# A decoder block with 32 experts on one core: whole 2 MB weight transfers in 16 KB rows, an eleventh buffer, and gather rows scaled on DVE

## The reference

```python
h = rms_norm(x, g_mix)
proj = h @ w_in                                  # 1024 x 9728: attention q/k/v, retention q/k/v/g, two gates
A = dilated window attention, three groups, 8 heads of 64
R = chunkwise retention, 4 heads, group norm, silu gate
x = x + (sigmoid(gA) * (A @ P_A) + sigmoid(gR) * (R @ P_R)) @ w_out
h2 = rms_norm(x, g_ffn)
# 4 expert groups of 8; the best group, the best 2 experts in it
y = sum over 32 experts e of
      gate[:, e] * ((silu(h2 @ w_gate[e]) * (h2 @ w_up[e])) @ w_down[e])
out = rms_norm(x + y, g_final)
```

## Time and profile before

| | us |
|---|---|
| median of 3 runs | 818.76 (817.61 to 819.12) |
| the profiled execution | 817.54 |
| its span | 815.8 |
| PE busy | 590.4 (72%) |
| PE weight loads | 420.7 (52%) |
| DVE busy | 248.7 (30%) |
| ACT busy | 198.7 (24%) |
| POOL busy | 20.7 (3%) |

### The profile page before, as it was taken

How to read it: one execution, slowest core, us unless ns; L and a number is a source line. 1 busy time by engine, 2 the same in 40 slices (tenths; PEclk the granted TensorE clock), 3 DMA queues, 4 the chain that set the end, 5 groups by cost and what they waited for, 6 DMA issues and landing times.

```text
span 815.8 us, 11861 instructions
## 1 busy us (share of the span) xinstructions
PE 590.4 (72%) x4469; PEld 420.7 (52%) x4469; DVE 248.7 (30%) x430; ACT 198.7 (24%) x292; POOL 20.7 (3%) x30
## 2 busy tenths in 40 slices
PE   3999999999999999955680780780770870960966
PEld 3999999999999998841320320320320320320311
DVE  6776574766664456460000000000000000000001
ACT  5454544565555433410000000000000000000001
POOL 3000000000000000120000000000000000000000
PEclk9999999999999999968795795795895895895888
DMA  7645526478786556889999999999999999999994
GB/s 209 163 112 144 155 80 181 133 235 247 241 263 199 182 187 228 329 358 378 415 414 422 415 415 421 417 415 421 418 415 419 419 415 419 419 417 418 419 412 175
DMA packets 111287, 255.82 MB, mean 314 GB/s; under 512 B 10017, under 2 KB 71457, under 8 KB 95649
## 3 DMA queue, kind: packets, MB, share of 16 engines
q1 hardware_dynamic: 109040, 255.36, 83.1%
q10 hardware_dynamic: 2224, 0.17, 0.2%
HBM read 254.45 MB, written 1.05 MB: 313 GB/s over the span
## 4 chain that ended last, share of the span: by engine, by line
PE 56%; DMA 21%; SPq 16%; DVE 2%; issue 2%; ACT 1%; DVEq 0%; ACTq 0%
PE ps L1040 56%; DMA ring<-in_w_down 20%; SPq L418 10%; SPq L427 6%; DMA gain<-in_g_mix 1%; ACT work L589 1%; DVE hn L717 1%; DVE rb L922 0%; DVE work L898 0%; PE ps L1119 0%; PE ps L1143 0%; DVE hn L1034 0%; ACT work L684 0%; DVE hT L725 0%; DVE split L693 0%
## 5 line engine op out<-in xcount | busy, mean ns | idle before, releaser
L1040 PE MATMUL ps<-store,work 128*32 128x512 f32 x128 | 75.1, 746 | 189.3 <-DMA ring<-in_w_down 189.2
L1040 PE MATMUL ps<-ring,work 128*32 128x512 f32 x896 | 188.4, 616 | 1.6 <-DVE work L972 0.9
L693 DVE TENSOR_TENSOR split<-ring,split 128x768 fp32r<-128x768 f32 (+2 forms) x132 | 120.5, 932 | 91.7 <-ACT split L541 91.1
L1040 PE MATMUL ps<-hT,split 128*128 128x256 f32 x1152 | 141.9, 285 | 2.0 <-DVE hT L725 2.0
L1040 PEld LDWEIGHTS ps<-hT,split 128*128 128x128 f32 x1152 | 140.3, 194 | 2.9 <-issue 2.4
L1040 PEld LDWEIGHTS ps<-store,work 128*32 128x32 f32 x128 | 15.8, 133 | 239.8 <-issue 224.7
L541 ACT ACTIVATE split<-ring 128x768 fp32r<-128x768 f32 (+2 forms) x132 | 107.1, 824 | 120.3 <-PE ps L1040 88.8
L1040 PE MATMUL ps<-mid,work 128*32 128x512 f32 x256 | 131.9, 671 | 0.0
L1040 PE MATMUL ps<-split,hT 128*128 128x256 f32 (+2 forms) x672 | 106.5, 316 | 0.0
L1040 PEld LDWEIGHTS ps<-split,hT 128*128 128x128 f32 x672 | 98.1, 190 | 4.4 <-issue 0.5
L972 DVE COPY work<-ps 128x512 f32<-128x512 f32 x8 | 5.5, 692 | 262.5 <-PE ps L1040 262.5
(11 more groups left out here) (175 smaller groups left out, 443.7 us busy)
## 6 DMA issues: line engine op xcount, KB each, us to landing
ring<-in_w_up SPq DMA_DIRECT2D x48, 1024.0 KB, 17.6
ring<-in_w_gate SPq DMA_DIRECT2D x42, 1024.0 KB, 21.6
ring<-in_w_in SPq DMA_DIRECT2D x96, 192.0 KB, 3.3
oRT_slot<-in_w_gate SPq DMA_DIRECT2D x16, 1024.0 KB, 20.7
mid<-in_w_up SPq DMA_DIRECT2D x16, 1024.0 KB, 14.7
store<-in_w_down SPq DMA_DIRECT2D x8, 2048.0 KB, 22.1
hT_slot<-in_w_down SPq DMA_DIRECT2D x8, 2048.0 KB, 26.7
mid<-in_w_down SPq DMA_DIRECT2D x32, 512.0 KB, 20.2
```

Source lines behind the costliest of these rows:

```text
L693: dve.tensor_tensor(split[:, s, 1, 0:n], raw(s, n), split[:, s, 0, 0:n].bitcast(F32), ALU.subtract).then_inc(lo_ready, 1)
L1040: return pe.matmul(o, lhsT=l, rhs=r, start=start, stop=stop, skip_group_check=shared)
```

## The change

- The source of the downs is laid out so that a partition takes four consecutive rows: 16 KB in one piece. The transposes of the hidden rows take every fourth column to match.
- Gates, ups and downs 0, 1, 2 are fetched whole (2 MB, rows of 16 KB). The first refill of the gates stays in halves. Down 3 comes in three pieces (1 MB in rows of 8 KB, then twice 512 KB in rows of 4 KB).
- An eleventh buffer, `spare`. `G_AT, U_AT, D_AT = (3, 4, 5, 10), (7, 0, 1, 2), (8, 9, 6, 0)`: gate 3 in the new one, down 2 in buffer 6, so only down 3 still shares (with up 1). Gate 3 of the first team is loaded in quarters in the retention loop, down 2 of the first team takes its place before the passes.
- SP waits for `gate_done` alone, and for `down_done1` alone; `down_half` is gone.
- `hn` is made by DVE in one instruction per tile, with root and gain; ACT's scaling and POOL's product are gone.
- `dynamic_dma_scratch_size=1024` makes room in SBUF.

```diff
+D3_PIECES = ((0, 2), (2, 3), (3, 4))
...
-    wd_v = w_down.rearrange("e (c p) d -> e p c d", p=P)
+    wd_v = w_down.rearrange("e (p c) d -> e p (c d)", p=P)
...
+        spare = sb("spare", [P, 4096])
...
-        G_AT, U_AT, D_AT = (3, 4, 5, 6), (7, 0, 1, 2), (8, 9, 7, 0)
+        G_AT, U_AT, D_AT = (3, 4, 5, 10), (7, 0, 1, 2), (8, 9, 6, 0)
...
                 quarter(5, wg_v[2][:, bass.ds(i * 1024, 1024)], i)
+                quarter(10, wg_v[3][:, bass.ds(i * 1024, 1024)], i)
...
+            def load_whole(p, view, at, js, loaded):
+
+                for j in js:
+                    sp.dma_start(slots[at[j]], expert(view, p, j)).then_inc(loaded, 16)
+
+            def load_last_down(p, n):
+
+                for m, (f, end) in enumerate(D3_PIECES):
+                    sp.wait_ge(up_done if m else up_half, n + 1)
+                    words = slice(f * D, end * D)
+                    sp.dma_start(slots[D_AT[3]][:, words], expert(wd_v, p, 3)[:, words]).then_inc(down3_loaded[m], 16)
...
+            def refill(p, q, n, first=False):
+
+                if first:
+                    for h, done in enumerate((gate_half, gate_done)):
+                        sp.wait_ge(done, 1)
+                        for j in range(TEAM):
+                            words = slice(h * 2048, (h + 1) * 2048)
+                            sp.dma_start(slots[G_AT[j]][:, words], expert(wg_v, q, j)[:, words]).then_inc(gate_loaded, 16)
+                else:
+                    sp.wait_ge(gate_done, n + 1)
+                    load_whole(q, wg_v, G_AT, range(TEAM), gate_loaded)
+                load_last_down(p, n)
+                load_whole(q, wu_v, U_AT, (0, 2, 3), up_loaded)
+                sp.wait_ge(down_done[1], n + 1)
+                load_whole(q, wu_v, U_AT, (1,), up_loaded)
+                load_whole(q, wd_v, D_AT, (0, 1, 2), down012_loaded)
...
+            passes = n_passes(sp)
+            refill(0, team_of(1), 0, first=True)
+            with sp.Fori(1, passes - 1) as n:
+                refill(team_of(n), team_of(n + 1), n)
+            load_last_down(NP - 1, passes - 1)
...
-            for t in range(TT):
-                act.activation(x2[:, t, :], x2[:, t, :], ACT.Copy, scale=rstd[:, 1, t:t + 1]).then_inc(x2_scaled, 1)
...
+            dve.wait_ge(s_gain, 32)
             for t in range(TT):
                 dve.wait_ge(rstd_done, TT + t + 1)
+                dve.scalar_tensor_tensor(hn[:, t, :, :], permuted(x2[:, t, :]), rstd[:, 1, t:t + 1], permuted(gain[:, :]),
+                                         ALU.mult, ALU.mult).then_inc(hn_done, 1)
...
-                    ins = pe.transpose(ps[:, 0, f * P:(f + 1) * P], hid[:, f * P:(f + 1) * P], ident[:, :])
+                    ins = pe.transpose(ps[:, 0, f * P:(f + 1) * P], hid[:, f:FF:FT], ident[:, :])
```

More of the change, by code:

```diff
@@ L242, in hybrid_block @@
         wr_ready = sem("wr_ready")
-        proj_done, x2_ev, x2_scaled = sem("proj_done"), sem("x2_ev"), sem("x2_scaled")
+        proj_done, x2_ev = sem("proj_done"), sem("x2_ev")
         raw_loaded = [sem(f"raw_loaded{s}") for s in range(CH)]
         hi_ready, lo_ready, chunk_used = sem("hi_ready"), sem("lo_ready"), sem("chunk_used")
[L246 to L249, removed]
+        gate_loaded, up_loaded = sem("gate_loaded"), sem("up_loaded")
+        down012_loaded = sem("down012_loaded")
+        down3_loaded = [sem(f"down3_loaded{m}") for m in range(len(D3_PIECES))]
         early = sem("early")
@@ L323, in parts @@
             return [split[:, s, a, 0:n].rearrange("p (k n) -> p k n", k=steps) for a in range(2)]
-        slots = [ring[:, s, :] for s in range(6)] + [oRT_slot[:, :], mid[:, :], store[:, :], hT_slot[:, :]]
-        G_AT, U_AT, D_AT = (3, 4, 5, 6), (7, 0, 1, 2), (8, 9, 7, 0)
+        slots = [ring[:, s, :] for s in range(6)] + [oRT_slot[:, :], mid[:, :], store[:, :], hT_slot[:, :],
+                                                         spare[:, :]]
+        G_AT, U_AT, D_AT = (3, 4, 5, 10), (7, 0, 1, 2), (8, 9, 6, 0)
         def n_passes(eng):
@@ L387, in quarter @@
             def quarter(slot, src, i):
-                sp.dma_start(ring[:, slot, bass.ds(i * 1024, 1024)], src).then_inc(early, 16)
+                sp.dma_start(slots[slot][:, bass.ds(i * 1024, 1024)], src).then_inc(early, 16)
             with sp.Fori(0, RET_HEADS) as i:
@@ L396, in _ @@
                 quarter(5, wg_v[2][:, bass.ds(i * 1024, 1024)], i)
-            for h in range(2):
-                sp.sem_inc(gate_loaded[h], 48)
+                quarter(10, wg_v[3][:, bass.ds(i * 1024, 1024)], i)
+            sp.sem_inc(gate_loaded, 64)
             with sp.Fori(0, GI) as i:
@@ L429, in _ @@
+            def load_last_down(p, n):
[3 more added lines that the diff above has]
+                    sp.dma_start(slots[D_AT[3]][:, words], expert(wd_v, p, 3)[:, words]).then_inc(down3_loaded[m], 16)
             sp.wait_ge(chunk_used, CH * (Q_WRET + 2))
-            for h in range(2):
-                load_halves(0, wg_v, G_AT, (3,), gate_loaded, h)
+            load_whole(0, wd_v, D_AT, (2,), down012_loaded)
@@ L432, in _ @@
             sp.wait_ge(b_ready, KT // 2)
-            for h in range(2):
-                load_halves(0, wu_v, U_AT, (0,), up_loaded, h)
+            load_whole(0, wu_v, U_AT, (0,), up_loaded)
             sp.wait_ge(lo_ready, CH * QUADS)
-            for h in range(2):
-                load_halves(0, wu_v, U_AT, (1,), up_loaded, h)
+            load_whole(0, wu_v, U_AT, (1,), up_loaded)
             sp.wait_ge(chunk_used, CH * QUADS)
-            for h in range(2):
-                load_halves(0, wu_v, U_AT, (2, 3), up_loaded, h)
@@ L441, in _ @@
-            for j in range(2):
-                load_down(0, j)
+            load_whole(0, wu_v, U_AT, (2, 3), up_loaded)
+            load_whole(0, wd_v, D_AT, (0, 1), down012_loaded)
             sp.wait_ge(hn_done, 2 * TT)
             sp.dma_start(gain[:, :], g_final.partition_broadcast(P)).then_inc(s_gain, 16)
[L446 to L451, removed]
+            def refill(p, q, n, first=False):
[13 more added lines that the diff above has]
+                load_whole(q, wd_v, D_AT, (0, 1, 2), down012_loaded)
@@ L453, in _, with team_of @@
             sp.wait_ge(sched_ready, 1)
             sp.wait_ge(order_ready, 1)
+            def team_of(n):
+                return sp.value_load(order[0:1, 0, bass.ds(n, 1)], min_val=0, max_val=NP - 1)
             passes = n_passes(sp)
[L456 to L469, removed]
@@ L653, in _ @@
                                ACT.Copy).then_inc(hT_act, 1)
-            for t in range(TT):
-                act.wait_ge(rstd_done, TT + t + 1)
-                act.activation(x2[:, t, :], x2[:, t, :], ACT.Copy, scale=rstd[:, 1, t:t + 1]).then_inc(x2_scaled, 1)
             for t in range(TT):
@@ L1283, in one_pass @@
                 pe.wait_ge(xg_dve, n + 1)
+                pe.wait_ge(gate_loaded, 64 if first else 64 * n + 128)
                 for h, done in enumerate((gate_half, gate_done)):
-                    pe.wait_ge(gate_loaded[h], 64 * n + 64)
                     team(2, w_gate, range(4 * h, 4 * h + 4), xg, slice(0, FF), KT).then_inc(done, 1)
```

32 lines of the change are left out of this document (8 added, 24 removed).

## The result

| | before | with the change |
|---|---|---|
| median (range, runs) | 818.65 (817.61 to 819.12, 4) | **811.53** (808.13 to 812.83, 4) |
| ratio, 95% interval | | **0.9909** (0.9893 to 0.9926) |
| profiled execution, its span | 817.54, 815.8 | 812.83, 811.1 |

The kernel is faster by 7.1 us, half of the 14.2 forecast; the time lies on the upper edge of the range (811.5).

A forecast was written before the change was run, and what follows sets the result against it. Bound: a PE-bound front, a short hand-over, then a DMA-bound weight stream. Terms -14.9 (stream), -4.0 (restart) and +4.7 (tail) sum to -14.2 us: 803.3 against the profiled execution, 804.6 predicted; range 800.5 to 811.5.

The forecast's parts named there:

- One weight fewer in the stream: Weight stream: fourth gate loaded in the retention, 178.26 MB instead of 180.36, -5.1 us; price in the front taken as 0.
- I take 0, since PE never stopped: Retention: four more 512 KB issues cost PE nothing, as converted chunks cover the longer wait; at most 5.1 us.
- rival 3: Retention: PE waits for converted chunks at the doubled extra, up to 5.1 us: 809.7; chance 0.09.
- Longer rows: Weight stream: 16 KB rows move at 429 GB/s, -14.9 us with the saved weight's 5.1 in it.
- the extrapolation: Weight stream: a 16 KB row takes 611.4 ns per DMA engine, from the times of 4 and 8 KB rows.
- the formula: Weight stream: 4 KB cost 150.4 ns per DMA engine, and each row 9.8 ns whatever its length.
- Rivals 1, 2 and 4: Stream: 16 KB rows as 8 KB (810.5, chance 0.20); rate by tensor (814.4, 0.06); long rows drag (822.0, 0.07).
- Scaling on DVE: Routing chain: without POOL's products DVE's L922 ends earlier, near 349.5, -3.3 us; DVE's own products cost 0.
- Hand-over: Before the first refill: three table loads moved ahead, -0.75; restart -4.0 us in all if the gather keeps 5.44 (bounds -1.6, +2.2).
- the prefetch isn't in the way: Before the first refill: the prefetch ended soon after 364 and gets some 0.7 us shorter.
- Coarser waits: Passes, at the wait for down_done1: 17.2 us of queued transfers cover PE's 9.0 and a 3.6 restart; 0 in all seven.
- The tail: After the last landing: PE's last down needs 9.0 us with 2.6 head start, ends 6.6 after landing, +4.7 us.

The follow-up runs named there:

- four other placements of the same weight: Against the changed kernel, gate 3's quarters in the gate loop 804.69; whole at front's end 804.99; quarters in attention loop 803.94; mid second quad of retention 805.24.
- the halves: Changed kernel with every whole 2 MB transfer issued as two of 1 MB in rows of 8 KB: 815.90 us.

## Why the prediction was right, and where it was not

- **One weight fewer in the stream, and its cost in the front.** The failed step is "I take 0, since PE never stopped". The front ends 6.8 us later, and four other placements of the same weight give it back. The prediction had the stall as rival 3, with a chance of 0.09, and its bound, 4 x 1.28 = 5.1, was too small as well. It priced the extra by its own bytes. What counts is how long the small piece behind two extras takes to land, 6.3 us here in place of 3.5, and how many turns it meets: three of four lost 1.9 to 2.3 us each. The size scatters: in the three profiled executions with this order (the changed kernel, the scaling undone on it, the halves) the second mean square stood at 349.91, 350.73 and 348.21, without it at 342.94 to 344.21. The evidence named for 0, PE without a gap, told that the cover was not used up, not how much of it was left. ACT's own wait of 2.54 us showed that a late piece was already using that cover.
- **Longer rows.** Right: 427 against 429 GB/s, and -14.3 against -14.9 for the stream. The 16 KB packets took 615 ns, the extrapolation said 611.4. Halves and quarters of a weight put 5.7 and 16.6 us back on the stream; the formula gives 5.9 and 17.4. Rivals 1, 2 and 4 are out.
- **Scaling on DVE.** Right: -3.15 against -3.3, with the named cause.
- **Hand-over.** The table loads gave 0.87 (forecast 0.75). The gather took 1.35 more, inside the bounds, with PE's clock low for most of it (the 6 in the 18th slice; from 360.04 to 366.83 its mean was 0.54, before, over the gather, 0.69). By the stall and this the refill came 4.2 later instead of 4.0 earlier. That the prefetch isn't in the way held, but barely: with the front in order it ended as the refill began.
- **Coarser waits.** Right: no dip in any pass (in windows of 2 us from 376 to 786 the DMA share never falls under 0.92); the awaited cover was never used up.
- **The tail.** +5.4 against +4.7. The last down took 9.8 us instead of 9.0: six groups and a part of a seventh ran at the low clock instead of the five taken from the earlier trace rows. (The prediction's own 9.0 less the 2.6 of head start is 6.4, not the 6.6 that it wrote; by the landing it came out at 7.4.)
- **The sum.** Without the stall the forecast was met: 804.69, 804.99, 803.94 and 805.24 in the four versions whose front has no gap, against 804.6. In the first of them it is met term by term, and not by errors that cancel: -4.3 to the first refill, -13.7 on the stream and +4.7 behind it, against -4.0, -14.9 and +4.7. What the 7.1 lack to 14.2 is the front's 6.8, and little else. That the changed kernel's time still fell on the edge of the range is luck: the upper edge was set by the prices of rivals 3 and 1 and a slow gather, and the stall cost more than rival 3 allowed.

## What to carry to other kernels

A transfer put into a stretch bound by another engine is priced by the delay of the latency-bound piece queued behind it, not by its bytes or the mean share of the DMA engines. Look at the longest wait of the first consumer, and avoid two big transfers in a row ahead of small ones that are soon needed: spread them, or put them where the consumer is far ahead. And a buffer that frees a piece of the stream moves the work behind the last landing: bring what ends last in step, in equal pieces.

## What the runs showed of the hardware

- A row has a fixed cost in the stream: 4, 8 and 16 KB rows took 163, 312 to 314 and 615 ns on a DMA engine, 410, 421 and 427 GB/s in all. From these three rates the fixed part is 8 to 9 ns a row, an estimate.
- A tiny instruction of POOL is held by a product on DVE too. Its second root (128x1, L487) took 2.40 us, before 0.56; DVE's first `hn` product (2.07 us, at 350.04) began in front of it, and with the scaling back on ACT and POOL the root took 0.56 again. The Trainium skill (SBUF — State Buffer, "SBUF: two separate sides") calls the port pair that the two share an exclusive lock, kept for the whole instruction: the runs agree, both ways, with DVE's `rb` at 3.77 against 0.17 in the other direction.
- The gather, 32 matmuls of one shape, took 5.30 to 6.79 us in the executions profiled here, and 3.84 in a pass. It goes with the granted clock: the mean over it was 0.71 in the shortest and 0.54 in the longest. It is the largest scatter left between the front and the stream.
